# Second gated feed-forward: the gate matmuls in the wide form, their two halves joined by ScalarE and VectorE

## The reference

```python
def conv_ffn(h, w_in, conv_w, conv_b, w_out):
    z = h @ w_in                                   # 1024 -> 2 * 2816
    u, g = z[..., :D_FF], z[..., D_FF:]            # values, gates
    a = causal_dwconv(u, conv_w) + conv_b          # three taps along the tokens
    return (jax.nn.silu(a) * g) @ w_out            # 2816 -> 1024

h = h + conv_ffn(rmsnorm(h, ffn_norm_g[layer]), ffn_w_in[layer], ffn_conv_w[layer], ffn_conv_b[layer], ffn_w_out[layer])
```

## Time and profile before

| | us |
|---|---|
| median of 3 runs | 1231.38 (1231.12 to 1231.49) |
| profiled execution, its own time | 1231.55 |
| its span | 1229.8 |
| PE busy | 1222.0 (99%) |
| DVE busy | 971.6 (79%) |
| ACT busy | 703.5 (57%) |
| POOL busy | 125.8 (10%) |

### The profile page before, as it was taken

One profiled execution on the slowest core, in us unless ns is written; L12 is line 12 of the kernel. 1 busy time (PEld: TensorE's weight loads), 2 busy tenths in 40 slices (PEclk: granted clock), 3 DMA queues, 4 the chain that ended last, 5 costly groups with the idle time before them and its releaser, 6 DMA issues.

```text
span 1229.8 us, 18608 instructions
## 1 busy us (share of the span) xinstructions
PE 1222.0 (99%) x7018; PEld 1063.2 (86%) x7018; DVE 971.6 (79%) x1234; ACT 703.5 (57%) x1061; POOL 125.8 (10%) x234
## 2 busy tenths in 40 slices
PE   9999999999999999999999999999999999999998
PEld 8989888888878988998999888888878998888887
DVE  5877999977976798898788778997784898676664
ACT  5555555657575555555777556555654253755552
POOL 2000000010011211111133101120010010000000
PEclk9999999999999999999999999999999999999999
DMA  9756777666553798893232358997565597385550
GB/s 305 251 163 213 244 246 235 227 207 187 192 170 103 246 334 309 314 334 116 74 106 71 135 181 291 392 392 247 187 212 200 172 318 264 118 292 191 186 187 35
DMA packets 154840, 265.80 MB, mean 216 GB/s; under 512 B 6108, under 2 KB 110675, under 8 KB 154774
## 3 DMA queue, kind: packets, MB, share of 16 engines
q1 hardware_dynamic: 136246, 205.29, 49.4%
q0 software_dynamic: 18352, 59.54, 14.0%
q10 hardware_dynamic: 176, 0.07, 0.0%
HBM read 263.79 MB, written 1.09 MB: 215 GB/s over the span
## 4 chain that ended last, share of the span: by engine, by line
PE 93%; DVE 4%; ACT 1%; POOL 1%; issue 0%; POOLq 0%; ACTq 0%
PE ps L2078 24%; PE ps L2058 18%; PE ps L2061 9%; PE ps L2042 4%; PE ps L2044 4%; PE ps L2043 4%; PE ps L2099 2%; PE ps L2101 2%; PE ps L2100 2%; PE ps L2121 2%; PE ps L2123 2%; PE ps L2122 2%; PE ps L2487 2%; DVE w_lo L1218 1%; PE ps L2178 1%; PE ps L2180 1%
## 5 line engine op out<-in xcount | busy, mean ns | idle before, releaser
L1218 DVE TENSOR_TENSOR w_lo<-raw,w_hi 128x2048 fp32r<-128x2048 f32 (+3 forms) x211 | 434.0, 2071 | 32.3 <-ACT w_hi L615 32.0
L615 ACT ACTIVATE w_hi<-raw 128x2048 fp32r<-128x2048 f32 (+3 forms) x213 | 368.6, 1737 | 51.2 <-PE ps L2078 43.5
L2058 PE MATMUL ps<-xn,w_hi 128*128 128x512 f32 x976 | 243.8, 392 | 0.0
L2058 PEld LDWEIGHTS ps<-xn,w_hi 128*128 128x128 f32 x976 | 178.2, 188 | 34.3 <-issue 0.4
L2061 PEld LDWEIGHTS ps<-xn,w_lo 128*128 128x128 f32 x976 | 133.1, 190 | 9.5
L2061 PE MATMUL ps<-xn,w_lo 128*128 128x256 f32 x976 | 136.1, 282 | 0.0
L2078 PE MATMUL ps<-w_hi,a_hi 128*128 128x512 f32 x432 | 134.6, 393 | 0.0
L695 ACT ACTIVATE work<-ps 128x512 f32<-128x512 f32 x61 | 36.3, 595 | 170.0 <-PE ps L2061 170.0
L2078 PE MATMUL ps<-w_lo,a_hi 128*128 128x512 f32 x432 | 133.5, 390 | 0.0
L2078 PE MATMUL ps<-w_hi,a_lo 128*128 128x512 f32 x432 | 133.2, 389 | 0.0
L2042 PE MATMUL ps<-xn,w_hi 128*128 128x256 f32 x432 | 122.8, 284 | 0.0
(11 more groups left out here) (378 smaller groups left out, 2004.0 us busy)
## 6 DMA issues: line engine op xcount, KB each, us to landing
raw<-in_ffn_w SPq DMA_DIRECT2D x64, 1024.0 KB, 5.5
side<-in_ada_w POOLq DMA_DIRECT2D x96, 512.0 KB, 6.2
raw<-in_ffn_w_in SPq DMA_DIRECT2D x40, 1024.0 KB, 5.2
raw<-in_ffn_w_out SPq DMA_DIRECT2D x32, 512.0 KB, 5.0
raw<-in_gm_w_in SPq DMA_DIRECT2D x16, 1024.0 KB, 6.1
raw<-in_od_w_in SPq DMA_DIRECT2D x12, 1024.0 KB, 5.9
raw<-in_gm_w_out SPq DMA_DIRECT2D x8, 1024.0 KB, 5.7
raw<-in_ev_w_in SPq DMA_DIRECT2D x6, 1024.0 KB, 13.0
```

Of the source, the lines that this page charges most:

```text
L615: nc.scalar.activation(w_hi[s][:, 0:w], raw[s][:, 0:w], ACT.Copy).then_inc(hi_done, 1)
L1218: nc.vector.tensor_tensor(w_lo[s][:, 0:w], raw[s][:, 0:w], w_hi[s][:, 0:w].bitcast(F32), ALU.subtract)\
L2058: nc.tensor.matmul(o, hi, xn[:, 512 * k:512 * k + 512], start=k == 0, stop=False)
```

## The change

For n = 1 the gates of steps 2 to 10 (nine tiles) are computed with `f_wide` into banks 2 and 3, as for n = 0. ACT copies one half behind the silu, DVE adds the halves ahead of its product, and the product reads the sum from SBUF where it read PSUM. The counts of the joins are moved up by the nine new ones.

```diff
-        J_RELU0 = J_FFN[1] + G_STEPS - 2
+        J_RELU0 = J_FFN[1] + 2 * G_STEPS - 4
 ...
                 def u_join(j):                     # on ACT and on DVE
-                    return j * 2 + (J_FFN[0] - 3) if n == 0 else j + (J_FFN[1] - 1)
+                    return j * 2 + (J_FFN[n] - 3)
 ...
                     nc.scalar.activation(f_s, wk(6144, 512), ACT.Silu).then_inc(g["silu"], 1)
-                    if j.c >= 2 and n == 0:
+                    if j.c >= 2:
                         act.wait_ge(w_used, val(u + 2))
                         low_copy(f_g, 2)
 ...
                     x = ps[3 if j.c == 0 else 1 if j.c == 1 else 2]
-                    if j.c >= 2 and n == 0:
+                    if j.c >= 2:
                         join(f_g, 2, u_join(j) + 1)
                         dve.wait_ge(join_done, val(u_join(j) + 1))
                         x = f_g
 ...
                         pe.wait_ge(g["prod"], val(j))
                         f_wide(u, 0)
-                        f_wide(u + 1, 2) if n == 0 else f_tile(u + 1, 2)
+                        f_wide(u + 1, 2)
```

## The result

The changed kernel takes 1238.51 us (median of 4 runs, 1238.22 to 1238.67), the kernel before 1231.38 (4 runs). That is 7.1 us more, a ratio of 1.0058 with a 95% interval of 1.0046 to 1.0070. The profiled execution took 1238.57 us with a span of 1236.9, 7.1 over the span of before.

What follows compares the result with a forecast made beforehand. DVE's sequence in the second feed-forward, already as long as PE's, was taken to set the end: 4.86 (steps 2 to 7) + 1.3 (8 and 9) + 1.15 (10) = 7.3 us, 1231.38 + 7.3 = 1238.7 us; range 1235.4 to 1242.7.

Steps and rivals of the forecast that it cites:

- DVE's own step: Second feed-forward's loop: DVE's step grows from 16.62 to 17.4 us, over PE's 16.61, waiting only for ACT's `a0`.
- The added pieces: Join and product's wait on DVE: 0.81 us a step in steps 2 to 7, 1.3 for 8 and 9, 1.15 for 10.
- The last product: DVE's last product of the second feed-forward, ahead of the transposes: 7.3 us later, and PE with it.
- the instruction alone: Rival: each join costs 0.6 us without its wait, nine make 5.4, 1236.8 us; half or less of it, 6%.
- No slack at the end: Stage's end: DVE's last product ends at 566.01, PE's transposes start at 566.07, so DVE's sequence is as long as PE's.
- PE's waits: PE waits some 0.8 us before the values of steps 7, 8 and 9, and 3.6 us before step 10's.
- the last wait: PE waits about 3 us before the transposes for DVE's last product.
- Half speed behind the wait before step 10: PE at half clock behind the 3.6 us wait: costs nothing, since PE has 3 us to spare there.
- A clock under 1.00 behind the waits: Sign that the prediction is wrong: windows behind PE's new waits show a granted clock under 1.00.
- The clock's rival: PE's clock falls in the new waits, about 2 us more behind the last: 1240.7 us, up to 1242.7; 15%.
- PE stays the bound: Second feed-forward behaves like the first: 1.6 us less, 1229.8 us, if a join costs DVE under 0.16 us a step; 7%.
- Late loads: DVE's later splits free buffers later, so loads are issued later: 1 us or more on top; 2%.

Runs made afterwards that it cites:

- the first experiment, e1_join_alone: Kernel before, gates still narrow on PE, but ACT's copy (scaled by 0) and DVE's join added from step 2 on: 1238.52 us, ratio 1.0055.
- the second experiment: Kernel before with wide gates on PE but no copy and no join, the product taking the first half alone: 1231.27 us, ratio 0.9997.
- the third: Changed kernel with wide gates and joins in steps 8 to 10 alone, narrow gates in the loop: 1235.57 us, ratio 1.0028.
- e7_step10_narrow: Changed kernel with a narrow tile and no join in step 10 alone: 1238.22 us, ratio 1.0051, in two groups.
- e3_last_three: Changed kernel with wide gates and joins in steps 8 to 10 alone: 1235.57 us, ratio 1.0028, in two groups.
- e10_spread_loads: Changed kernel with two of four modulation sums a step moved behind the values' join and four side loads issued earlier, folds left in step 9: 1231.97 us.
- e8_all_moves: Changed kernel with two modulation sums a step moved behind the values' join, step 9's folds moved into waits for ACT, four side loads earlier: 1229.7 us.
- e5_spread_and_folds: Changed kernel with two modulation sums a step moved behind the values' join and step 9's folds moved into waits for ACT: 1234.38 us, ratio 1.0023.

## Why the prediction was right

The forecast was 1238.7 us, measured were 1238.51.

**DVE's own step.** Predicted 17.4 us with only the wait for `a0` in it; measured 17.41 with 1.43. That this step, and not anything on PE, makes the loss is shown by the first experiment: with the copy and the join alone it is all there.

**The added pieces.** 0.81 us a step in the loop: measured 3.01 - 2.20 = 0.81. The last product: predicted 7.3 us later, measured 7.12. The rest came short in the loop, where DVE's split of step 8 moved by 536.41 - 531.72 = 4.69 us and not by 4.86. Reading the price of a sequence from the other layer, which had it already, gave it with the waits that belong to it; the instruction alone (0.6 us) would have given 5.4.

**No slack at the end.** This was read from two rows, 566.01 against 566.07, and is shown by the second experiment (PE's saving gives nothing) and the third (three joins at the end are paid in full).

**PE's waits.** Predicted were some 0.8 us before steps 7, 8 and 9; PE's steps are 0.77, 0.91 and 0.53 us over 16.61. Before step 10 3.6 were predicted and the row says 3.17, with the end of the matmul ahead of it modelled: from 549.14 + 0.95, where the last eight matmuls of the tile before should have ended, to 553.42 it is 3.3. The step that failed is the last wait: I put 3 us before the transposes and there is none to speak of. Half speed behind the wait before step 10 was weighed in the prediction, as costing nothing because PE had 3 us to spare. It came, it cost PE 2.95 us in the trace, and so it ate that very wait. A clock under 1.00 behind the waits was also one of the signs by which the prediction said that it would be wrong, and by that sign it was wrong on the clock. The time is right in spite of it, with 0.1 us to spare, and that is luck: nothing in the sum said that the fall would cost less than PE had to spare. `e7_step10_narrow` shows how near it was: with DVE 1.1 us earlier PE has no time left even behind the shorter fall.

**The clock's rival** (2 us more, 15%) is half true: the clock fell in a new wait, but not in the last, where it would have been paid. In the trace the first fall left no last wait for it. In the executions with a mean of 1.000 there should have been one of up to 3 us, and their times are no longer; no trace shows them. In `e3_last_three` and `e10_spread_loads` the slower groups have the rival's mark, 1.6 to 1.7 us more for an estimate of 2, so that the changed kernel was spared it may be luck too.

**PE stays the bound** (1229.8 us, 7%) was the rival on the other side, and the point at which I said it decides was DVE finding its time in the 1.42 us wait. `e8_all_moves` makes DVE find it there (with the folds and the loads moved as well), and the time is 1229.7. **Late loads** (2%) did not come: no wait of DVE in the stage's loop is for a load.

## What to carry to other kernels

Before giving the busiest engine's work to a second engine, cut the second one's timeline into steps and sort its waits: a wait for the first engine is room, a round trip to a third engine is part of its step, and no lead pays for it. Look also where the two sequences meet last; if they arrive within 0.1 us of each other, shortening one gives nothing and lengthening the other costs in full. Filling a round trip with work that is there anyway is the way to make such a change pay, but each moved instruction has to be followed back to the load that it reads.

## What was not expected of the hardware

PE's granted clock fell to 0.50 at waits for which the forecast had put nothing: of 3.17 us in the changed kernel, and also of 2.2 us in `e5_spread_and_folds`, by their traces. It cost PE 2.95 us in the changed kernel and 1.68 us in the traces of `e1_join_alone`, `e7_step10_narrow` and `e5_spread_and_folds`. With a last wait of 2.7 us (`e3_last_three`) the mean clock was lower in four of seven executions, with one of 1.9 us (`e10_spread_loads`) in five of eleven, with 1.7 and 1.6 us more. So one and the same kernel has two times, some 1.7 us apart. Only the traces of the quicker group were taken there, and they have 1.00 behind the wait; that the half clock of the slower one stands behind this very wait is argued from its mean and its price, not shown. What decides between the two stays open. In these runs such a fall is paid only where PE is the chain behind the wait: in the changed kernel it cost PE 2.95 us and the program nothing that can be measured.
